# Two more neighbourhood heads mixed feature-major with split value weights in a two-block transformer kernel

## The chip, the cores and the metric

One NeuronCore of one Trainium2 chip runs the whole program. The metric is the device time of one execution in microseconds (us). The engines are TensorE (PE in the profile; its weight loads are PEld), VectorE (DVE), ScalarE (ACT), GpSimd (POOL) and SyncE (SP, which here only starts DMAs). Each engine runs its own instructions strictly in order and waits for the others by semaphores.

## The reference

The input is 256 tokens of width 1024. A first block and then a second one are computed in float32. Only the attention of the second block is touched here:

```python
u = rms_norm_2(h, mix_norm[l]);  z = u @ w_in[l]
qa, ka, va, qb, kb, vb, ga, gb = split(z)
ya = neighbourhood_attention_2d(qa, ka, va, rpb)       # 8 heads of 64: softmax(q k^T * scale + bias) v
yb = windowed_gqa_sink(rope(qb), rope(kb), vb, sink)   # 8 heads of 64, 2 key/value groups
merged = sigmoid(ga) * (ya @ w_branch_a) + sigmoid(gb) * (yb @ w_branch_b)
h = h + merged @ w_out
```

A neighbourhood head is thus a 256x256 score matrix, a softmax over each row, and the product of the probabilities with 256x64 values.

## The kernel before

**Numbers in two halves.** Float32 matmuls are done on values split into a high half (rounded to f32r by a copy on ACT) and a low half (the rest, subtracted on DVE). A product is then three f32r matmuls: high by high, high by low, low by high (`three`, lines 694 to 697). Weights arrive in panels of 1 MB in a ring of three (`raw`); ACT makes the high half of a panel (`hi`, line 1332), DVE the low half (`lo`, line 1802), each two panels ahead of PE. SP starts the load of a panel when DVE has made the low half of the panel three before it.

**The stretch.** The change lies in the projection stage of block 2, panels QKV2 to BR-1, which are called panels 0 to 16 here: QA2 = 0 and 4, KA2 = 1 and 5, VA2 = 2 and 3, KBVB = 6, QB = 7 and 8, GA2 = 9 to 12, GB2 = 13 to 16. Panels 0, 1 and 4 to 8 are of 48 matmuls 128x256 in two halves of 24; panels 2, 3 and 9 to 16 of 24 matmuls 128x512 with a break in the middle. The 16 attention heads are put between the halves of these panels by a table written by hand: slot 2p is the middle of panel p, slot 2p+1 its end (`places`, line 675). Head k has one slot for its scores (`score2`), a later one for turning its probabilities (`turn2_`) and a later one for its product with the values (`mix2`). In one slot PE does mix, turn and score in this order. Heads 0 to 7 are the neighbourhood heads, 8 to 15 the windowed ones.

**The two ways of a head.** `FV = 6` divides them. A head under FV: DVE masks the scores (`mask2`), ACT takes the exponential and the row sums (`exp2`), PE turns four 128x128 blocks of probabilities by float32 transposes, ACT copies them out of PSUM (`copy2`, into `probT2`), and PE does four float32 matmuls, turned probabilities as weights, 64 columns of values moving (line 1239; the profile counts each as two). The result is token-major; DVE takes the reciprocal of the sums and scales it into `atok2` (`norm2`). A head from FV on: DVE scales the probabilities by the reciprocal before they are turned (`scale2`, one slot behind the score's), ACT copies the turned ones as high half (`copy2` into `pth`), DVE makes the low half (`low_probs`), and PE does four f32r matmuls (line 1229) with 128 columns of weights, the 64 high and 64 low columns of the value side by side, and 256 columns of probabilities moving. The result is feature-major in two rows of 64 partitions; ACT copies the lower 64 (`low_rows`), DVE adds them to the upper ones (`norm2`). The mix waits for `low_probs` of its head.

**Order on DVE and ACT.** Both run through the panels too. DVE at n: take panel n-1 out of PSUM with its scale; the head work of slot (n-1, end): mask, low half of the probabilities, norm, scale; `lo(n+2)`; rope of panel n-1 where it was queries or keys of the windowed heads; at panel 8 the low halves of these keys (line 2394); the head work of slot (n, middle); at panel 8 then the low half of `vb` (line 2407). ACT at n, up to panel 9: `hi(n+2)`; high halves of queries; `swap` of the rope (line 1636), which waits until DVE has taken the panel out; then `low_rows` and `copy2` of slot (n-1, end), the exponentials of that slot, and `copy2` of slot (n, middle). From panel 10 on `low_rows` and `copy2` come first.

**Buffers and end.** `atok2` of heads 4 and 5 is turned by two transposes on PE after panel 12 (line 1296) into the third 128 rows of `midh`, `midl`; heads 6 and 7 need none, being written to `y3`.

Of the kernel before, what the change touches and what calls it, by code (L numbers as in the profile page):

```python
# [14 lines left out]
F32 = mybir.dt.float32  # L15
F32R = mybir.dt.float32r
ALU = mybir.AluOpType
ACT = mybir.ActivationFunctionType
AX_X = mybir.AxisListType.X

P = 128
T = 256
TT = T // P
D = 1024
KT = D // P
DH = 64
NH = 8
GR = 2
NC = 15
# [3 lines left out]
PW = 2048  # L33
R = 3
# [19 lines left out]
KBVB, QB, GA2, GB2 = QKV2 + 6, QKV2 + 7, QKV2 + 9, QKV2 + 13  # L54
# [45 lines left out]
def build(nc, a, out):  # L100
    ctx = ExitStack()
    with ctx:
        def sb(name, shape, dt=F32):
            return ctx.enter_context(nc.sbuf_tensor(name, shape, dt))
# [6 lines left out]
        wh_all = sb("wh", [P, R * PW + KT * 24], F32R)  # L111
        wl_all = sb("wl", [P, R * PW + KT * 24], F32R)
# [4 lines left out]
        midh = sb("midh", [P, 6, T], F32R)  # L117
        midl = sb("midl", [P, 6, T], F32R)
# [4 lines left out]
        xs = sb("xs", [P, TT, D])  # L123
        vec = sb("vec", [P, V_ALL])
        cw2 = sb("cw2", [P, 2, 2, DH])
        hid = sb("hid", [P, 2, 2, 2 * NC])
        hidt = sb("hidt", [P, 2 * CH])
        ssq = sb("ssq", [P, 2 * TT])
        wsq = sb("wsq", [P, 2 * TT])
# [19 lines left out]
        def carve(at, *shape):  # L149
            n = int(np.prod(shape))  # L150
            v = arena[:, at:at + n]
            names = "abcd"[:len(shape)]
            if len(shape) == 1:
                return v
            return v.rearrange("p (%s) -> p %s" % (" ".join(names), " ".join(names)),
                               **{k: s for k, s in zip(names, shape)})
# [18 lines left out]
        vblk = hidt[:, :].rearrange("p (g r d) -> p g r d", g=GR, r=4)  # L175
        pc = xsf[:, 1536:2048].rearrange("p (t h n) -> p t h n", t=TT, h=NH)
        pcT = carve(8224, 4, P)
        kcd = sb("kcd", [P, GR, 2 * NC])
        thr = sb("thr", [P, T])
        nth = carve(9760 + T, T)  # L180

# [6 lines left out]
        va = carve(10240, TT, NH * DH)  # L188
# [5 lines left out]
        pth, ptl = mrgl[:, 4:6, :], mrgl[:, 6:8, :]  # L194
        ylow = thr
        y3 = carve(12544, T)
        vns = midl[:, 4:6, :].rearrange("p k t -> p (k t)").rearrange("p (k h s d) -> p k h s d", k=TT, h=2, s=2)
        vbs = midh[:, 4:6, :].rearrange("p k t -> p (k t)").rearrange("p (k g s d) -> p k g s d", k=TT, g=GR, s=2)
        atok2 = carve(14336, TT, NH * DH)
        ybT = xs[:, 0, :].rearrange("p (k t) -> p k t", t=T)  # L200
# [20 lines left out]
        ps = [pair01[:, i, :] for i in range(2)] + [acc4[:, i, :] for i in range(4)] + [pair67[:, i, :] for i in range(2)]  # L221

        ident = cst[:, C_ID:C_ID + P]
# [99 lines left out]
        normed = sem("normed")  # L323
        atok_turned = sem("atok_turned")
        midh_ready = sem("midh_ready")
        midl_ready = sem("midl_ready")
# [317 lines left out]
        def head2(k):  # L644

            h = k % NH
            if k < NH:
                kh, kl = keys2(h // 4)
                return (qst[:, h, :], kh[:, h % 4, :], kl[:, h % 4, :],
                        [va[:, kt, DH * h:DH * (h + 1)] for kt in range(TT)] if h < FV else  # L650
                        [vns[:, kt, h - FV, :, :].rearrange("p s d -> p (s d)") for kt in range(TT)])
            g = h // 4
            return (qst[:, h, :], mrgl[:, g, :], mrgl[:, GR + g, :],
                    [vbs[:, kt, g, :, :].rearrange("p s d -> p (s d)") for kt in range(TT)])
# [7 lines left out]
            return ps[TURNED[0]][:, 0:T] if j == 3 else ps[3][:, 0:T]  # L662

        OUT_A = 5
        FV = 6
        KEY_BANKS = (KSKW % 2, 2)
        V_BANKS = (6, 5)
        LOW, HIGH, LAST = (0, 1), (4, 5), (6, 7)
# [8 lines left out]
        def places(slots):  # L677

            return {(QKV2 + at // 2, at % 2): k for k, at in enumerate(slots)}
# [1 line left out]
        SCORE_SLOTS = (5, 7, 9, 11, 13, 15, 17, 19, 21, 22, 23, 25, 26, 27, 29, 30)  # L681
        score_at = places(SCORE_SLOTS)
        scale_at = places([at + 1 for at in SCORE_SLOTS])
        turn_at = places((7, 9, 11, 13, 15, 17, 20, 22, 23, 25, 26, 27, 28, 30, 31, 32))
        mix_at = places((9, 11, 13, 15, 17, 19, 21, 23, 25, 26, 27, 28, 29, 31, 32, 33))


# [1 line left out]
        def _(pe):  # L689
# [274 lines left out]
            for c in range(2):  # L964
                m = high_first(1, c, ps[1][:, c * T:(c + 1) * T])
            m.then_inc(panel_done, 1)
            for n in range(KCVC, UPA):
# [3 lines left out]
                if n in CMPS:  # L971

                    s, u = CMPS.index(n) // 2, CMPS.index(n) % 2
                    if n == CMPS[0]:
                        pe.wait_ge(flatl_ready, 1)
                    h, l = pv(n, KT, wh), pv(n, KT, wl)
# [8 lines left out]
                elif n == VSVW:  # L985
                    h, l = vg(vg_h), vg(vg_l)
# [13 lines left out]
                else:  # L1000
                    for c in range(2):
                        out_ = ps[KEY_BANKS[c]][:, 0:T] if n == KSKW else bank1(n)[:, c * T:(c + 1) * T]
                        m = high_first(n, c, out_)
# [263 lines left out]
            for n in range(QKV2 + 1, BR):  # L1267
                split(n)
                free_bank2(n)
                if n in col2:  # L1270
                    for c in range(2):
                        m = feature_tile(n, KT, c, ps[n % 2][:, c * T:(c + 1) * T], acth, actl)
                        if c == 1:
                            m.then_inc(panel_done, 1)
                        elif n == QKV2 + 1:
                            spread(3)
                        heads2(n, c)
                else:
                    u = (n - (VA2 if n < GA2 else GA2)) % 4
                    token_panel(n, GATE2_BANKS[u // 2], acth, actl, 4 * (u % 2), u % 2 == 0, u % 2 == 1,  # L1280
                                lambda: heads2(n, 0)).then_inc(panel_done, 1)
                    heads2(n, 1)
                if n == QB:
                    pe.wait_ge(kv_evac, 1)
                    for tt in range(TT):
                        m = nc.tensor.transpose(ps[OUT_A][:, tt * P:(tt + 1) * P], vbT[:, tt * P:(tt + 1) * P], ident)
                    m.then_inc(vb_turned, 1)
                if n == GA2:
                    pe.wait_ge(normed, NH + 4)
                    pe.wait_ge(vb_ready, 1)  # L1290
                    turn_out(OUT_A, atok2, 0)
                if n == GA2 + 3:
                    pe.wait_ge(normed, NH + FV)
                    pe.wait_ge(midl_ready, 2)
                    for tt in range(TT):
                        m = nc.tensor.transpose(ps[OUT_A][:, tt * P:(tt + 1) * P], atok2[:, tt, 2 * P:3 * P], ident)
                    m.then_inc(atok_turned, 1)

            for u in range(2):
                for br, (ah, al) in enumerate(((midh, midl), (acth, actl))):  # L1300
# [14 lines left out]
        def _(act):  # L1315
# [368 lines left out]
            for n in range(QKV2, F2):  # L1684
# [42 lines left out]
                                             scale=rstd[:, tt:tt + 1]).then_inc(va_evac, 1)  # L1727
                if n == VA2 + 3:
                    act.wait_ge(va_evac, 2)
                    nc.scalar.activation(vns[:, :, :, 0, :], va[:, :, DH * FV:DH * NH].rearrange("p k (h d) -> p k h d", h=2),  # L1730
                                         ACT.Copy).then_inc(vnh_ready, 1)
                if n - 1 in (QB, QB + 1):
                    u = n - 1 - QB
# [17 lines left out]
                if n in (GA2 + 1, GA2 + 4):  # L1751
                    if n == GA2 + 1:
                        out_hi(midh, 0, OUT_A, 2)
                    else:
                        act.wait_ge(atok_turned, 3)
                        nc.scalar.activation(midh[:, 2, :], ps[OUT_A][:, 0:T], ACT.Copy)
                        act.wait_ge(normed, 2 * NH)
                        nc.scalar.activation(midh[:, 3, :], y3, ACT.Copy).then_inc(midh_ready, 1)
                if not grouped:
                    gates2(n)  # L1760
# [28 lines left out]
        def _(dve):  # L1789
# [498 lines left out]
            def norm2(k):  # L2288
                if k >= FV:

                    dve.wait_ge(ylow_ready, k - FV + 1)
                    to = y3 if k < NH else ybT[:, (k - NH) // 2, :]
                    nc.vector.tensor_tensor(to[own(k % 2)], ps[4][0:DH, 0:T], ylow[0:DH, :],
                                            ALU.add).then_inc(normed, 1)
                    return
                dve.wait_ge(mixed, NH + k + 1)
                o = k % 3
                c = coef[:, o, 0:TT]
                link(nc.vector.reciprocal(c, sums[:, o, 0:TT]))
                for tt in range(TT):  # L2300
                    m = nc.vector.tensor_scalar(atok2[:, tt, DH * k:DH * (k + 1)], ps[4][:, tt * DH:(tt + 1) * DH],
                                                coef[:, o, tt:tt + 1], None, ALU.mult)
                m.then_inc(normed, 1)
# [31 lines left out]
            for n in range(QKV2, F2):  # L2335
# [64 lines left out]
                    queries_lo(qbT, u, 5 + u)  # L2400
                if n == VA2 + 3:
                    dve.wait_ge(vnh_ready, 1)
                    nc.vector.tensor_tensor(vns[:, :, :, 1, :], va[:, :, DH * FV:DH * NH].rearrange("p k (h d) -> p k h d", h=2),
                                            vns[:, :, :, 0, :].bitcast(F32), ALU.subtract).then_inc(vn_ready, 1)
                if n == QB + 1:
                    dve.wait_ge(vbh_ready, 1)
# [2 lines left out]
                if n in (GA2 + 1, GA2 + 4):  # L2409
                    if n == GA2 + 1:  # L2410
                        out_lo(midl, midh, 0, OUT_A, 2)
                    else:
                        dve.wait_ge(midh_ready, 3)
                        nc.vector.tensor_tensor(midl[:, 2, :], ps[OUT_A][:, 0:T], midh[:, 2, :].bitcast(F32), ALU.subtract)
                        nc.vector.tensor_tensor(midl[:, 3, :], y3, midh[:, 3, :].bitcast(F32), ALU.subtract).then_inc(midl_ready, 1)

            residual(4, F2 - 1, then=V_F2)
# [73 lines left out]
```

## Time and profile before

| what | value |
|---|---|
| time, median of 3 runs | 952.55 us (952.55 to 952.73) |
| time of the profiled execution | 952.4 us |
| its span, first to last instruction | 950.5 us |
| mean granted TensorE clock | 0.999 |
| PE busy | 943.2 us (99%) |
| DVE busy | 665.9 us (70%) |
| ACT busy | 536.3 us (56%) |

A busy share is of the whole span; shares of single stretches differ much from it. The 1.9 us between the span and the time of the profiled execution lie outside the recorded instructions. All moments below are us from the start of the span.

### The profile page before, as it was taken

What the parts mean: (1) busy time and instruction counts of PE and PEld (TensorE: products, weight loads), DVE (VectorE), ACT (ScalarE), POOL (GpSimd) and SP (SyncE); (2) the same over time, 40 slices, a digit from 0 to 9 for tenths busy, and PEclk for the clock granted to TensorE, in tenths of its full rate; (3) what the DMA queues carried; (4) which work ended last, traced back from release to release, by engine and by line L of the source; (5) the groups of instructions that cost most, each with busy time, mean ns of one, the idle gap of its engine ahead of it and who ended that gap; (6) DMA issues with size and microseconds to landing.
All of it is one profiled execution on the core that took longest, in us unless ns stands there. A gap on an engine that the chain in (4) does not pass through costs nothing.

```text
span 950.5 us, 13952 instructions
## 1 busy us (share of the span) xinstructions
PE 943.2 (99%) x5400; PEld 826.7 (87%) x5400; DVE 665.9 (70%) x857; ACT 536.3 (56%) x691; POOL 62.3 (7%) x95
## 2 busy tenths in 40 slices
PE   9999999999999999999999999999999999999997
PEld 8999988888888888898888888999888898888886
DVE  7888869876655565688666666878887586665665
ACT  7687688535444444474454445679674465444544
POOL 1200000002000000022221000100100020000000
PEclk9999999999999999999999999999999999999999
DMA  9785335553756555547666655545435555655541
GB/s 304 227 244 168 110 123 182 199 178 118 273 181 197 199 177 184 187 160 243 207 207 204 201 177 177 181 137 170 133 133 178 177 192 185 220 178 183 194 153 44
DMA packets 119471, 173.14 MB, mean 182 GB/s; under 512 B 3168, under 2 KB 91488, under 8 KB 119424
## 3 DMA queue, kind: packets, MB, share of 16 engines
q1 hardware_dynamic: 117904, 168.41, 54.9%
q0 software_dynamic: 1376, 3.81, 1.4%
q8 instruction: 33, 0.54, 0.2%
q10 hardware_dynamic: 144, 0.26, 0.1%
q14 instruction: 14, 0.11, 0.0%
HBM read 171.42 MB, written 1.05 MB: 181 GB/s over the span
## 4 chain that ended last, share of the span: by engine, by line
PE 99%; DVE 0%; ACT 0%; issue 0%
PE pair L726 22%; PE pair L729 11%; PE acc L695 10%; PE acc L697 10%; PE acc L696 10%; PE pair L695 6%; PE pair L697 6%; PE pair L696 6%; PE pair L713 2%; PE pair L717 2%; PE pair L714 2%; PE acc L1065 1%; PE pair L923 1%; PE acc L1214 1%; PE acc L853 1%; PE pair L871 1%
## 5 line engine op out<-in xcount | busy, mean ns | idle before, releaser
L726 PE MATMUL pair<-actp,wh 128*128 128x512 f32 x912 | 292.8, 396 | 0.0
L1806 DVE TENSOR_TENSOR wl<-raw,wh 128x2048 fp32r<-128x2048 f32 x89 | 204.8, 2303 | 62.7 <-ACT wh L1338 62.7
L1338 ACT ACTIVATE wh<-raw 128x2048 fp32r<-128x2048 f32 x88 | 168.3, 1913 | 84.1 <-PE acc L697 84.1
L729 PEld LDWEIGHTS pair<-actp,wl 128*128 128x128 f32 x912 | 171.3, 188 | 40.0
L729 PE MATMUL pair<-actp,wl 128*128 128x256 f32 x912 | 179.2, 278 | 0.0
L1802 DVE TENSOR_TENSOR wl<-raw,wh 128x2048 fp32r<-128x2048 f32 x68 | 155.6, 2291 | 31.3 <-ACT wh L1332 30.9
L1332 ACT ACTIVATE wh<-raw 128x2048 fp32r<-128x2048 f32 x69 | 132.1, 1916 | 70.9 <-PE pair L697 27.4
L726 PEld LDWEIGHTS pair<-actp,wh 128*128 128x128 f32 x912 | 141.6, 189 | 1.4
L1553 ACT ACTIVATE arena<-pair 128x512 f32<-128x512 f32 x57 | 34.1, 598 | 170.8 <-PE pair L726 170.8
L695 PE MATMUL acc<-wh,midh 128*128 128x512 f32 x310 | 120.9, 390 | 0.0
L697 PE MATMUL acc<-wh,midl 128*128 128x512 f32 x310 | 120.6, 389 | 0.0
L696 PE MATMUL acc<-wl,midh 128*128 128x512 f32 x310 | 120.6, 389 | 0.0
L2153 DVE TENSOR_TENSOR arena<-pair,arena 128x512 f32<-128x512 f32 x57 | 39.4, 692 | 90.2 <-ACT arena L1553 90.2
L696 PEld LDWEIGHTS acc<-wl,midh 128*128 128x128 f32 x310 | 58.2, 188 | 12.2
L697 PEld LDWEIGHTS acc<-wh,midl 128*128 128x128 f32 x310 | 58.2, 188 | 12.2
L695 PEld LDWEIGHTS acc<-wh,midh 128*128 128x128 f32 x310 | 58.2, 188 | 10.7
L695 PE MATMUL pair<-wh,actp 128*128 128x512 f32 x160 | 63.6, 398 | 0.0
L697 PE MATMUL pair<-wh,actp 128*128 128x512 f32 x160 | 62.5, 391 | 0.0
L696 PE MATMUL pair<-wl,actp 128*128 128x512 f32 x160 | 62.4, 390 | 0.0
L2142 DVE TENSOR_TENSOR midl<-xs,midh 128x512 fp32r<-128x512 f32 x38 | 26.5, 698 | 23.1 <-ACT midh L1556 23.1
L713 PE MATMUL pair<-actp,wh 128*128 128x256 f32 x168 | 42.3, 290 | 0.0
L714 PE MATMUL pair<-actp,wh 128*128 128x256 f32 x168 | 41.1, 283 | 0.0
(375 smaller groups left out, 1452.3 us busy)
## 6 DMA issues: line engine op xcount, KB each, us to landing
raw<-in_w_in SPq DMA_DIRECT2D x35, 1024.0 KB, 5.2
raw<-in_mlp_w SPq DMA_DIRECT2D x32, 1024.0 KB, 5.2
raw<-in_ffn_w_gate SPq DMA_DIRECT2D x22, 1024.0 KB, 5.4
raw<-in_ffn_w_up SPq DMA_DIRECT2D x22, 1024.0 KB, 5.4
raw<-in_ffn_w_down SPq DMA_DIRECT2D x22, 1024.0 KB, 5.0
raw<-in_w_out SPq DMA_DIRECT2D x8, 1024.0 KB, 4.9
raw<-in_w_up_rnn SPq DMA_DIRECT2D x4, 1024.0 KB, 5.2
raw<-in_w_in SPq DMA_DIRECT2D x5, 512.0 KB, 5.5
```

The source lines that it names most:

```text
L695: nc.tensor.matmul(out_, lh, rh, start=start, stop=False, **kw)
L696: nc.tensor.matmul(out_, lh, rl, start=False, stop=False, **kw)
L697: return nc.tensor.matmul(out_, ll, rh, start=False, stop=stop, **kw)
L713: nc.tensor.matmul(out_, h[:, k, cs], acth[:, k, :], start=k == 0, stop=False)
L714: nc.tensor.matmul(out_, h[:, k, cs], actl[:, k, :], start=False, stop=False)
L726: return nc.tensor.matmul(bank[:, :].rearrange("p (u t) -> p u t", u=2), h[:, k, cs], actp[:, :, k, :], **kw)
L729: return nc.tensor.matmul(bank[:, 0:T], l[:, k, cs], acth[:, k, :], **kw)
L1332: nc.scalar.activation(to, src, ACT.Copy).then_inc(hi_ready, 1)
L1338: nc.scalar.activation(wh[:, slot(n), :], raw[:, slot(n), :], ACT.Copy).then_inc(hi_ready, 1)
L1802: nc.vector.tensor_tensor(to, src, high.bitcast(F32), ALU.subtract).then_inc(lo_ready, 1)
L1806: nc.vector.tensor_tensor(wl[:, slot(n), :], raw[:, slot(n), :], wh[:, slot(n), :].bitcast(F32), ALU.subtract).then_inc(lo_ready, 1)
L2153: return nc.vector.tensor_tensor(r, pair[:, :, 0:T], r, ALU.add)
```

## The change

FV becomes 4: heads 4 and 5 go the second way. Their values are split too: four copies on ACT and four subtractions on DVE at panel 5 in place of one each. Head 4's value weights lie in the unused last columns of `wh_all` and `wl_all`, head 5's in a new tile. Their turns move half a panel later, from slots 15 and 17 to 16 and 18; the slots of the scores and mixes stay. The result of the two heads goes to `y2`, so that the two transposes after panel 12 and their two waits go; ACT and DVE read `y2` in SBUF instead of a PSUM bank. `hid` and `kcd` of block 1 move into the shared arena.

```diff
-        FV = 6
+        FV = 4
-        turn_at = places((7, 9, 11, 13, 15, 17, 20, 22, 23, 25, 26, 27, 28, 30, 31, 32))
+        turn_at = places((7, 9, 11, 13, 16, 18, 20, 22, 23, 25, 26, 27, 28, 30, 31, 32))
+        y2 = carve(14592, T)
+        vn5 = sb("vn5", [P, TT, P], F32R)
+        vn4 = [v[:, R * PW:R * PW + P] for v in (wh_all, wl_all)]
...
                         [va[:, kt, DH * h:DH * (h + 1)] for kt in range(TT)] if h < FV else
-                        [vns[:, kt, h - FV, :, :].rearrange("p s d -> p (s d)") for kt in range(TT)])
+                        vn4 if h == 4 else [vn5[:, kt, :] for kt in range(TT)] if h == 5 else
+                        [vns[:, kt, h - 6, :, :].rearrange("p s d -> p (s d)") for kt in range(TT)])
...  (PE)
-                if n == GA2 + 3:
-                    pe.wait_ge(normed, NH + FV)
-                    pe.wait_ge(midl_ready, 2)
-                    for tt in range(TT):
-                        m = nc.tensor.transpose(ps[OUT_A][:, tt * P:(tt + 1) * P], atok2[:, tt, 2 * P:3 * P], ident)
-                    m.then_inc(atok_turned, 1)
...  (ACT, n == VA2 + 3; DVE subtracts in the same four pieces)
-                    nc.scalar.activation(vns[:, :, :, 0, :], va[:, :, DH * FV:DH * NH].rearrange("p k (h d) -> p k h d", h=2),
+                    for kt in range(TT):
+                        nc.scalar.activation(vn4[kt][:, 0:DH], va[:, kt, DH * 4:DH * 5], ACT.Copy)
+                    nc.scalar.activation(vn5[:, :, 0:DH], va[:, :, DH * 5:DH * 6], ACT.Copy)
+                    nc.scalar.activation(vns[:, :, :, 0, :], va[:, :, DH * 6:DH * NH].rearrange("p k (h d) -> p k h d", h=2),
                                          ACT.Copy).then_inc(vnh_ready, 1)
...  (ACT, n == GA2 + 4)
-                        act.wait_ge(atok_turned, 3)
-                        nc.scalar.activation(midh[:, 2, :], ps[OUT_A][:, 0:T], ACT.Copy)
                         act.wait_ge(normed, 2 * NH)
+                        nc.scalar.activation(midh[:, 2, :], y2, ACT.Copy)
...  (DVE, norm2)
-                    to = y3 if k < NH else ybT[:, (k - NH) // 2, :]
+                    to = (y2, y3)[k // 2 - 2] if k < NH else ybT[:, (k - NH) // 2, :]
```

## Rows read from the trace of the kernel before

**Rows 1.** The page: busy time, share of the span and instructions of each engine.
```profile
PE 943.2 (99%) x5400; PEld 826.7 (87%) x5400; DVE 665.9 (70%) x857; ACT 536.3 (56%) x691; POOL 62.3 (7%) x95
```

**Rows 2.** Waits of PE's weight loads, 590 to 760: total us, times, longest.
```profile
PEld acc L1199 <- issue: 0.4, 1, 0.4
```

**Rows 3.** Timeline of PE (start us, busy us, engine, line, operation), 645 to 669.
```profile
646.40 0.61 PE L1214 MATMUL acc<-cst,arena 128*128 128x128 f32 x4
646.76 0.36 PE L1199 MATMUL acc<-midh,mrgh 128*128 128x256 f32 x1
...
647.46 0.36 PE L695 MATMUL pair<-actp,wh 128*128 128x256 f32 x1
...
653.29 1.00 PE L1239 MATMUL acc<-arena 128*128 128x64 f32 x8
654.13 0.60 PE L1214 MATMUL acc<-cst,arena 128*128 128x128 f32 x4
...
655.05 0.39 PE L695 MATMUL pair<-wh,actp 128*128 128x512 f32 x1
...
660.52 1.00 PE L1239 MATMUL acc<-arena 128*128 128x64 f32 x8
...
668.28 0.64 PE L1229 MATMUL acc<-mrgl,midl 128*128 128x256 f32 x4
668.76 0.28 PE L1199 MATMUL acc<-mrgl,mrgh 128*128 128x256 f32 x1
```

**Rows 4.** Timeline of DVE, 630 to 672, with the idle time before an instruction.
```profile
630.74 0.69 DVE L2348 TENSOR_TENSOR arena<-pair,arena 128x512 f32<-128x512 f32 x1 [1.85 <-PE pair L697]
...
644.28 0.42 DVE L2327 TENSOR_TENSOR arena<-xs 128x256 f32<-128x256 f32 x1
645.76 0.69 DVE L2343 SCALAR_TENSOR_TENSOR arena<-pair,arena 128x512 f32<-128x512 f32 x1 [1.06 <-PE pair L697]
...
648.81 2.28 DVE L1802 TENSOR_TENSOR wl<-raw,wh 128x2048 fp32r<-128x2048 f32 x1
651.01 0.69 DVE L2324 TENSOR_TENSOR xs<-arena,cst 128x512 f32<-128x512 f32 x1
...
652.94 1.71 DVE L2394 TENSOR_TENSOR mrgl<-arena,mrgl 64x256 fp32r<-64x256 f32 x4
654.68 0.42 DVE L2407 TENSOR_TENSOR midh<-acc,midh 128x256 fp32r<-128x256 f32 x1
...
661.17 0.16 DVE L2276 RECIPROCAL coef<-sums 128x2 f32<-128x2 f32 x1
...
662.02 1.39 DVE L1896 TENSOR_TENSOR mrgh<-arena,mrgh 64x512 fp32r<-64x512 f32 x2
...
666.92 0.68 DVE L2285 TENSOR_TENSOR mrgl<-acc,mrgl 128x512 fp32r<-128x512 f32 x1
...
671.19 0.41 DVE L2293 TENSOR_TENSOR arena<-acc,thr 64x256 f32<-64x256 f32 x1
```

**Rows 5.** Timeline of ACT, 631 to 669, with the idle time before an instruction.
```profile
631.46 2.59 ACT L1702 ACTIVATE midh<-arena 64x512 fp32r<-64x512 f32 x4 [3.20 <-DVE arena L2348]
...
648.39 2.55 ACT L1636 ACTIVATE arena<-arena 32x512 f32<-32x512 f32 x4
...
651.25 0.59 ACT L1625 ACTIVATE arena<-acc 128x512 f32<-128x512 f32 x1
...
653.55 1.92 ACT L1332 ACTIVATE wh<-raw 128x2048 fp32r<-128x2048 f32 x1 [0.59 <-PE pair L697]
...
656.65 2.56 ACT L1636 ACTIVATE arena<-arena 32x512 f32<-32x512 f32 x4
...
668.96 0.38 ACT L1631 ACTIVATE thr<-acc 64x256 f32<-64x256 f32 x1 [2.13 <-PE acc L1229]
```

**Rows 6.** Stretches of 1 us at the end: length, busy of each engine, PEclk.
```profile
944.00:945.00 1.00, 0.49 (x5) 0.29 (x3) 0.85 (x2) 0.97 (x4) 0.35 (x1) 1.00 0.00 0
...
948.00:949.00 1.00, 0.00 (x0) 0.00 (x0) 0.00 (x0) 0.00 (x0) 0.00 (x0) 0.75 1.03 391
```

More of the change, by code:

```diff
@@ L125, in build @@
         cw2 = sb("cw2", [P, 2, 2, DH])
-        hid = sb("hid", [P, 2, 2, 2 * NC])
         hidt = sb("hidt", [P, 2 * CH])
@@ L177, in build @@
         pcT = carve(8224, 4, P)
-        kcd = sb("kcd", [P, GR, 2 * NC])
+        hid = carve(15392, 2, 2, 2 * NC)
+        kcd = carve(15512, GR, 2 * NC)
         thr = sb("thr", [P, T])
@@ L2402, in _ @@
                     dve.wait_ge(vnh_ready, 1)
-                    nc.vector.tensor_tensor(vns[:, :, :, 1, :], va[:, :, DH * FV:DH * NH].rearrange("p k (h d) -> p k h d", h=2),
+                    for kt in range(TT):
+                        nc.vector.tensor_tensor(vn4[kt][:, DH:P], va[:, kt, DH * 4:DH * 5], vn4[kt][:, 0:DH].bitcast(F32), ALU.subtract)
+                    nc.vector.tensor_tensor(vn5[:, :, DH:P], va[:, :, DH * 5:DH * 6], vn5[:, :, 0:DH].bitcast(F32), ALU.subtract)
+                    nc.vector.tensor_tensor(vns[:, :, :, 1, :], va[:, :, DH * 6:DH * NH].rearrange("p k (h d) -> p k h d", h=2),
                                             vns[:, :, :, 0, :].bitcast(F32), ALU.subtract).then_inc(vn_ready, 1)
@@ L2413, in _ @@
                         dve.wait_ge(midh_ready, 3)
-                        nc.vector.tensor_tensor(midl[:, 2, :], ps[OUT_A][:, 0:T], midh[:, 2, :].bitcast(F32), ALU.subtract)
+                        nc.vector.tensor_tensor(midl[:, 2, :], y2, midh[:, 2, :].bitcast(F32), ALU.subtract)
                         nc.vector.tensor_tensor(midl[:, 3, :], y3, midh[:, 3, :].bitcast(F32), ALU.subtract).then_inc(midl_ready, 1)
```

## The prediction

> **What bounds the kernel now.** First the page's busy shares: PE is busy for 99% of the span [rows 1], so a microsecond of PE work saved or waited for anywhere is a microsecond of the whole. Then PE's waits over the attention stage: the only entry is 0.4 us in one piece that nothing releases [rows 2]; no head makes PE wait now. Then the timelines of PE, DVE and ACT side by side, since the change gives DVE and ACT more work here and puts a new wait into PE. The reader is to see two things. PE's head work sits between panel matmuls without a hole [rows 3]. On DVE, from 648.81 on, `lo`, rope (651.01), the low key halves (652.94) and `vb`'s low half (654.68) stand end to end, with no idle time shown before any of them [rows 4]. ACT in the same panels holds two swaps of 2.55 us, at 648.39 and 656.65 [rows 5]. DVE's 70% over the span [rows 1] hides this full stretch.
>
> **PE work, removed and moved.** An old mix takes 653.29 to 654.13 = 0.84 us, a new one 668.28 to 668.76 = 0.48 us [rows 3]: two heads save 2 x 0.36 = 0.72. The four transposes of a turn take 646.40 to 646.76 = 0.36 [rows 3]; the two transposes that go are half of that, 0.18. The moved turns are the same work. Where float32 work hands over to f32r the first matmul is longer (0.36 against 0.28 for the same shape [rows 3]); two such switches go (a new mix is followed by scores of its own kind) and two come (a turn alone in the middle of a panel), so I cost them at nothing, bounds -0.2 to +0.2. Sum for PE: -0.9 us, bounds -0.7 to -1.1.
>
> The Trainium skill bears on this term ("TensorE: Matmul & The Clock Gate", section "Back-to-back issue gap"). Its formula for isolated matmuls, columns / 2.4 plus 2.5 ns, with its floor of 25 ns, would give the old mix 8 x 29 ns = 0.23 us and the new one 4 x 109 ns = 0.44, so the change would cost 0.4 us in place of saving 0.7. The trace disagrees for the small ones: 0.84 us for eight is 105 ns each [rows 3]. The same section says that the formula counts too little at few columns because every matmul has its weight load, and by that the trace agrees. The rows are used.
>
> **Work hidden at panel 5.** The four value copies and four subtractions replace one each. Nearest rows: 0.38 us for an ACT copy of 256 columns [rows 5], 0.41 for a DVE operation of 256 [rows 4]; eight operations of at most that size are under 3.3 us, six of them new; as the pieces have 64 to 128 columns I take 0.6 us more on ACT and 0.5 on DVE. Behind them DVE idles 1.85 us until 630.74 [rows 4] and ACT 3.20 until 631.46 [rows 5]. Cost 0; were that cover gone, the next mask and `copy2` would be up to a microsecond late, three panels ahead of the heads in question. Moving `hid` and `kcd`, and reading `y2` from SBUF instead of PSUM, costs nothing either: same operations, far from PE's next need. Bounds of all these -0.1 to +0.3.
>
> **The scale of head 4.** `scale2(4)` comes on DVE behind rope's last piece (644.28 + 0.42 = 644.70) and takes 661.17 to 662.02 = 0.85. DVE idles 1.06 there before 645.76 [rows 4]: hidden, with 0.2 to spare.
>
> **First new wait: mix of head 4 at slot 17.** When PE gets there: panel 8 starts at 647.46 now and its end is 653.29 [rows 3]. The turn leaves slot 15 (-0.36) and comes into the middle of panel 8 with its switch (+0.44): 653.37. What it waits for is `low_probs(4)`. On ACT, the swap from 648.39 ends at 650.94 as now, and then exponential and `copy2(4)` stand in the other order; both are done when ACT now falls idle, 653.55 - 0.59 = 652.96 [rows 5]. That is in time. DVE is not: the low half of the probabilities comes behind the low key halves in program order, so not before 654.68, where `vb` now starts [rows 4]. Can DVE be earlier? Its mask of head 5 comes 0.36 earlier, as the turn ahead of its scores is gone, but rope then waits for ACT's swap, over at 650.94, and rope starts at 651.01 already [rows 4, 5]. So DVE's time stands. `low_probs` takes 0.68 [rows 4]: done 655.36, with an allowance of 0.1 for handing over 655.46. **PE stands for 2.1 us.** Bounds 1.4 (0.3 lost or gained in either chain, twice) to 2.8. Behind the waiting mix on PE are the scores of head 6 and all of panel 9.
>
> **Second new wait: mix of head 5 at slot 19.** PE: 655.46, mix 0.48, scores 0.48 (the same four matmuls of 256 columns), panel 9 660.52 - 655.05 = 5.47 [rows 3], turn with switch 0.44: 662.3. DVE: behind `low_probs(4)` (next start 655.28) come `scale2(5)` 0.85 and `vb`'s low half, 0.34 to the next start: 656.5; then taking out panel 8, 0.65: 657.1. Only now may ACT swap (now it starts at 656.65, behind other ACT work, so ACT is ready): 657.2 + 2.56 = 659.75 [rows 5]. Behind the swap in ACT's order stands `low_rows(4)`, 0.38 [rows 5]: 660.15. DVE's `norm2(4)` waits for that, and behind it on DVE are queued `lo` of panel 11, rope and `low_probs(5)`: 660.15 + 0.4 + 2.2 (648.81 to 651.01) + 1.93 (651.01 to 652.94) + 0.68 = 665.35 [rows 4], handed over 665.45. **PE stands for 3.1 us.** The wait of DVE for `low_rows` is the dear part, about 2.3 us (657.8 after the mask, to 660.15): an old head's norm needs PE alone. Bounds 2.0 to 4.2, as six terms add.
>
> **What is late next.** PE's lag is now 665.45 - 660.52 - 0.36 = 4.6 us. DVE's: `scale2(6)`, now at 661.17, comes at 665.3, a lag of 4.1. As DVE lags less than PE, and `low_probs(6)` ends now at 667.60 for a mix at 668.28 [rows 3, 4], 0.7 to spare, head 6 and all behind it keep their distances. Queries and high halves move by no more. No third wait (bounds 0 to 0.4). Later SP's load of panel 14 starts some 4 us later, behind `lo` of panel 11; two panels of distance cover it, and if they didn't, PE would wait for up to 4 us more.
>
> **Sum**, against the profiled execution, 952.4 (its span 950.5 and 1.9 around it): -0.9 + 2.1 + 3.1 = +4.3, so 956.7. The median before is 0.15 above that execution: **956.8**.
>
> **Rivals.**
> A, *no new wait; only PE's saving is left*. It decides at one point: whether `low_probs(4)` is done by 653.4 and `low_probs(5)` by PE's 660.2. For it: the exponential and the copy are done at 652.96. Against it: DVE's row at 654.68 and its program order. Price: -0.9, so 951.6, not slower.
> B, *only the first wait*. `norm2(4)` would have to find `low_rows(4)` done, so DVE reaches `low_probs(5)` at 657.1 + 0.7 + 0.4 + 2.2 + 1.93 = 662.3, done 663.1: a wait of 0.8 in place of 3.1, 954.5, or with none 953.7. Against it: the 2.56 us swap ahead of `low_rows`.
> C, *the waits cool the clock*. PE's last work ends near 944.5, and the granted clock still reads 1.00 up to 948 and 0.75 in the microsecond after it [rows 6], so it fell to the 1.2 GHz level after some 3.5 us of standing; my second wait is 3.1. Price: a panel of 5.47 us [rows 3] at half rate is +5.5 at most, I take half: 959.5. The Trainium skill states such a rule, under "HAM oscillation — how this bites in real kernels" of "TensorE: Matmul & The Clock Gate": TensorE that stands idle long enough for data drops back to the lower clock and starts its next work cold. By the page a single wait could bring this time; by the rows here, mine is just short of what did.
> D, *faster by more than PE's saving*, through some wait in the panels not seen in rows 2: none speaks for it.
>
> **Chances.** Forecast 0.70 (955.3 to 958.5), B 0.10, A 0.08, C 0.07, D and the unforeseen 0.05. Range 953.4 to 959.2: it takes in B and the lower half of C, and leaves A and the dearest of C out. A measurement of this kernel can tell 0.2%, 1.9 us, from no change: faster means under 950.7, slower over 954.4. Faster 0.06 (D, and part of A), same 0.14 (A, half of B), slower 0.80.
>
> **What the changed profile would show.** PE's waits: a line for `pth`/`ptl` behind L2285 on DVE, twice, about 2 and 3 us, ahead of the mixes of heads 4 and 5; the four matmuls of those mixes at 0.48 a head. DVE: `low_probs` near 654.7 directly behind the low key halves, and an idle time of about 2.3 us before `norm2(4)`, released by ACT. ACT: no time lost before its second swap but that until 657.2. If PE shows no wait, DVE's order was read wrongly and A holds; if the second wait is missing, the chain through swap and `low_rows` is wrong; if PEclk dips near 665, C.

## The result, and the profile after

The changed kernel takes 956.56 us (median of 6 runs, 956.32 to 957.92), the kernel before 952.55 (6 runs, 952.27 to 953.18): a ratio of 1.0043, 95% interval 1.0032 to 1.0053. It is slower by 4.0 us; 956.8 was predicted. The profiled execution took 956.65 us with a span of 954.9, 4.4 more than the span before. In this kernel's listing the lines of PE have moved down by four: 699 to 701 for `three`, 1218 the turns, 1233 the f32r mixes; those of ACT's head work have moved up by two (`swap` 1634, `low_rows` 1629, `copy2` 1623).

The page, first part, against [rows 1]: PE's busy time grows by 1.0 us, though its work has become less, and there are ten rows fewer.

```profile
PE 944.2 (99%) x5390; PEld 827.2 (87%) x5390; DVE 668.7 (70%) x864; ACT 536.9 (56%) x696; POOL 61.6 (6%) x95
```

Waits of PE's weight loads, 590 to 760 (engine and line, what released it: us in total, times, longest), against the single line of [rows 2]. The two new ones stand ahead of the mixes of heads 4 and 5. Their releaser is named "issue" here. The timelines name DVE for the second; for the first it is inferred from the times, as `low_probs(4)` ends at 654.76 + 0.69 = 655.45 and the mix starts at 655.56.

```profile
PEld acc L1233 <- issue: 3.8, 2, 2.2
PEld acc L1203 <- issue: 0.4, 1, 0.4
```

Timeline of PE (start us, busy us, engine, line, operation, idle before), which answers to [rows 3]. The end of panel 8, mix and scores, the first half of panel 9, its turn, its end, the mix of head 5 with its scores, and the mix of head 6:

```profile
653.29 0.28 PE L701 MATMUL pair<-actp,wl 128*128 128x256 f32 x1
655.56 0.77 PE L1233 MATMUL acc<-mrgl,wh 128*128 128x256 f32 x2 [1.99 <-issue]
656.12 0.63 PE L1233 MATMUL acc<-mrgl,wl 128*128 128x256 f32 x2
...
657.40 0.63 PE L699 MATMUL pair<-wh,actp 128*128 128x512 f32 x1
...
660.83 0.60 PE L1218 MATMUL acc<-cst,arena 128*128 128x128 f32 x4
...
663.79 0.39 PE L701 MATMUL pair<-wh,actp 128*128 128x512 f32 x1
665.42 0.71 PE L1233 MATMUL acc<-mrgl,vn 128*128 128x256 f32 x4 [1.24 <-DVE mrgl L2285]
...
672.84 0.64 PE L1233 MATMUL acc<-mrgl,midl 128*128 128x256 f32 x4
```

The reader is to see three things: the mix of head 4 starts 2.15 us after its turn has come (653.29 + 0.12, one matmul's distance), the mix of head 5 1.4 us after (663.79 + 0.23), and between them PE is slow: from 657.40 to the turn it takes 3.43 us for what took 2.75 where the clock was high (e8 below, 656.22 to 658.97). At the mix of head 6 the lag behind [rows 3] is 672.84 - 668.28 = 4.56 us.

Timeline of DVE, which answers to [rows 4]. `scale2(4)` stands in the old idle time; `low_probs(4)` (L2285) is directly behind the low key halves; `norm2(4)` idles DVE for 1.71 us until ACT's `low_rows`; `low_probs(5)` closes the chain:

```profile
644.71 0.16 DVE L2276 RECIPROCAL coef<-sums 128x2 f32<-128x2 f32 x1
...
645.85 0.69 DVE L2343 SCALAR_TENSOR_TENSOR arena<-pair,arena 128x512 f32<-128x512 f32 x1 [0.33 <-PE pair L701]
...
653.02 1.71 DVE L2394 TENSOR_TENSOR mrgl<-arena,mrgl 64x256 fp32r<-64x256 f32 x4
654.76 0.69 DVE L2285 TENSOR_TENSOR mrgl<-acc,mrgl 128x512 fp32r<-128x512 f32 x1
...
660.13 0.42 DVE L2293 TENSOR_TENSOR arena<-acc,thr 64x256 f32<-64x256 f32 x1 [1.71 <-ACT thr L1629]
660.47 2.27 DVE L1802 TENSOR_TENSOR wl<-raw,wh 128x2048 fp32r<-128x2048 f32 x1
...
664.59 0.68 DVE L2285 TENSOR_TENSOR mrgl<-acc,mrgl 128x512 fp32r<-128x512 f32 x1
```

Timeline of ACT, which answers to [rows 5]: the second swap waits for DVE, `low_rows(4)` follows it.

```profile
657.14 2.55 ACT L1634 ACTIVATE arena<-arena 32x512 f32<-32x512 f32 x4 [0.41 <-DVE arena L2343]
659.71 0.38 ACT L1629 ACTIVATE thr<-acc 64x256 f32<-64x256 f32 x1
```

Stretches of 1 us (length, busy of PE, PEld, DVE, ACT and POOL, PEclk, DMA share, GB/s). The third figure from the end is the granted clock: 0.50 is the 1.2 GHz level, 1.00 the 2.4 GHz level, and a figure between them is the mean of a microsecond in which it changed. The 0.73 puts the fall near 655.46, at the very end of PE's first wait; the clock was back in the course of 658 to 659.

```profile
654.00:655.00 1.00, 0.00 (x0) 0.00 (x0) 0.96 (x3) 1.00 (x1) 0.00 (x0) 1.00 1.05 410
655.00:656.00 1.00, 0.44 (x2) 0.47 (x3) 0.96 (x4) 1.00 (x2) 0.00 (x0) 0.73 0.35 133
656.00:657.00 1.00, 1.00 (x7) 1.00 (x7) 1.00 (x3) 0.72 (x2) 0.00 (x0) 0.50 0.00 0
...
658.00:659.00 1.00, 1.00 (x4) 0.78 (x3) 0.41 (x4) 0.99 (x2) 0.00 (x0) 0.56 0.00 0
```

### The profile page after: what moved, and what is told of

It is laid out like the page before. It is cut to its first block, busy times and chain, and to the rows that moved or that the text cites. A ratio compares the mean times of both kernels' runs of the same rounds, so it can differ in the third digit from the quotient of the medians.

```text
span 954.9 us, 13945 instructions
## 1 busy us (share of the span) xinstructions
PE 944.2 (99%) x5390; PEld 827.2 (87%) x5390; DVE 668.7 (70%) x864; ACT 536.9 (56%) x696; POOL 61.6 (6%) x95
## 4 chain that ended last, share of the span: by engine, by line
PE 96%; DVE 2%; ACT 1%; DMA 1%; issue 0%; SPq 0%
PE pair L730 22%; PE pair L733 11%; PE acc L699 10%; PE acc L701 10%; PE acc L700 10%; PE pair L699 5%; PE pair L701 5%; PE pair L700 5%; PE pair L721 2%; PE pair L717 2%; PE pair L718 2%; PE acc L1069 1%; PE pair L927 1%; PE acc L857 1%; PE acc L1218 1%; DMA raw<-in_w_in 1%
```

## The experiments

The theory: PE's time at the mix of head 5 is set by one chain on DVE and ACT (low key halves, `low_probs(4)`, taking out panel 8, second swap, `low_rows(4)`, `norm2(4)`, `lo`, rope, `low_probs(5)`), whatever PE did before. The rivals: the fall of the clock is a part of the loss; DVE simply has too much work, in any order. Each kernel was timed in five rounds, beside the kernel before on the same chip: 952.30 us beside e1 to e4, 952.39 beside e5 to e8, 952.60 beside e9.

**e1: the first wait filled with matmuls that nobody reads.**

```diff
             def mix2(k):
                 vt = head2(k)[3]
+                if k == 4:
+                    for _ in range(5):
+                        nc.tensor.matmul(ps[6][:, 0:T], ident, cst[:, C_COS:C_COS + T], start=True, stop=True)
```

> The changed kernel with five float32 matmuls 128x256, whose result nobody reads, put on PE ahead of the mix of head 4, so that PE works through most of its first wait of 2.1 us and its clock does not fall. Chain theory: what sets the end is the chain on DVE and ACT up to the low half of head 5's probabilities (near 665.3), whatever PE does before; the second wait grows from 1.4 to about 3 us, PEclk stays at 1.0, the time stays at 956.5 (956.2 to 957.0). Clock theory: the stretch at 1.2 GHz from 655.4 to 658.6 is part of the loss; without it the time falls by about 1.5 us to 955.0.

Measured: 957.79 us, ratio 1.0052 (1.0039 to 1.0066). The clock stayed high through the first wait, and as the chain theory has it, the mix of head 5 starts at the same moment all the same (665.23), now after 2.75 us of idle. But the time is 0.8 above the range I gave. One of the five executions took 956.30, the others 957.69 to 958.17; the trace is of one of these. PE's timeline and the clock behind this second wait:

```profile
665.23 0.71 PE L1236 MATMUL acc<-mrgl,vn 128*128 128x256 f32 x4 [2.75 <-DVE mrgl L2288]
...
674.22 0.64 PE L1236 MATMUL acc<-mrgl,midl 128*128 128x256 f32 x4
```

```profile
665.00:666.00 1.00, 0.77 (x6) 0.80 (x7) 0.93 (x5) 0.03 (x1) 0.00 (x0) 1.00 1.00 385
666.00:667.00 1.00, 1.00 (x9) 1.00 (x7) 0.99 (x2) 1.00 (x2) 0.00 (x0) 0.61 0.96 373
667.00:668.00 1.00, 1.00 (x5) 0.81 (x4) 0.97 (x5) 1.00 (x1) 0.00 (x0) 0.50 0.05 16
```

The clock now falls here, with PE at work again, and nothing behind it takes the loss up: from the mix of head 5 to that of head 6 it is 8.99 us (674.22 - 665.23), in the changed kernel 7.42 (672.84 - 665.42).

**e8: both waits filled.** As e1, and six more such matmuls into a free bank ahead of the mix of head 5.

```diff
+                if k == 5:
+                    pe.wait_ge(qb_evac, 2)
+                for _ in range({4: 5, 5: 6}.get(k, 0)):
+                    nc.tensor.matmul(ps[6 if k == 4 else 0][:, 0:T], ident, cst[:, C_COS:C_COS + T], start=True, stop=True)
```

> The changed kernel with unread matmuls in both waits (five ahead of head 4's mix, six ahead of head 5's), so that the clock falls behind neither. Chain theory: PE starts the mix of head 5 at the same moment as in the changed kernel and goes on at the full clock: 956.5 (956.1 to 956.9), 1.3 less than with the first wait alone filled (957.8). If the added 1.3 us there came from something else than the clock: 957.8 again.

Measured: 956.20 us, ratio 1.0039 (1.0026 to 1.0053), inside the range; the clock reads 1.00 in both places.

```profile
655.19 0.47 PE L1237 MATMUL acc<-mrgl,wh 128*128 128x256 f32 x2
...
656.22 0.40 PE L699 MATMUL pair<-wh,actp 128*128 128x512 f32 x1
658.97 0.60 PE L1218 MATMUL acc<-cst,arena 128*128 128x128 f32 x4
...
665.06 0.71 PE L1237 MATMUL acc<-mrgl,vn 128*128 128x256 f32 x4
...
672.47 0.64 PE L1237 MATMUL acc<-mrgl,midl 128*128 128x256 f32 x4
```

Two things follow. One fall of the clock with nothing behind it to hide it costs 957.79 - 956.20 = 1.59 us, and the rows say the same (8.99 - 7.41 = 1.58). And with no fall at all the loss is still 956.20 - 952.39 = 3.8 us: the fall in the changed kernel was all but free (956.56 - 956.20 = 0.36 us, or 0.2 when each is taken against the kernel before beside it). There the mix of head 4, scores and half a panel took 660.83 - 655.56 = 5.27 us against 658.97 - 655.19 = 3.78 here; these 1.5 us were taken from the second wait, not added to the end.

**e2: head 4's lower rows ahead of the second swap on ACT.**

```diff
+                if n == GA2:
+                    heads2_turned(n - 1, 1)
                 if n - 1 in (QB + 1, QB + 2):
...
-                if not grouped:
+                if not grouped and n != GA2:
                     heads2_turned(n - 1, 1)
```

> The changed kernel with the copy of head 4's lower rows ahead of the rope's second swap on ACT, in place of behind it. Chain theory: norm2(4) no longer idles DVE for 1.7 us, low_probs(5) is done near 663.5 in place of 665.3, and PE, which arrives near 664.0 with the low clock behind it, doesn't wait a second time: 956.5 - 1.4 = 955.1. Work theory (DVE simply has too much to do in this stretch, and the order is of no account): no change, 956.5.

Measured: 954.16 us, ratio 1.0020 (1.0011 to 1.0029), 2.4 less than the changed kernel. `norm2(4)` no longer idles DVE, `low_probs(5)` starts 2.6 us earlier, and PE comes later than it:

```profile
657.31 0.41 DVE L2295 TENSOR_TENSOR arena<-acc,thr 64x256 f32<-64x256 f32 x1
...
661.98 0.68 DVE L2287 TENSOR_TENSOR mrgl<-acc,mrgl 128x512 fp32r<-128x512 f32 x1
```

```profile
663.72 0.64 PE L1233 MATMUL acc<-mrgl,vn 128*128 128x256 f32 x4
```

The same work in another order, so the work rival falls for this part. The gain is larger than I said, by 0.9. The executions fall into two groups, and the mean granted clock of each execution tells them apart: six of 953.93 to 954.16 us with 0.998 to 1.000, and five of 954.63 to 954.89, all with 0.996. The profiled one is of the upper group; in its trace PEclk is 0.50 from 657 to 659. Some 3 us at half rate lower the mean of such a span by about 0.002 (an estimate from these figures), so in the faster group the clock seems not to have fallen behind the same wait of 2 us. The groups are 0.8 us apart, less than a whole fall costs by e8, since PE without the fall reaches the mix before `low_probs(5)` is done (e5 below shows 0.55 us of wait there).

**e3: head work of panel 8's middle ahead of the low key halves on DVE.**

```diff
+                heads2(n, 0)
                 if n == QB + 1:
                     dve.wait_ge(kst_hi, 9)
...
                     m.then_inc(kst_ready, 1)
-                heads2(n, 0)
```

> The changed kernel with the head work of the middle of panel 8 on DVE (low half of head 4's probabilities, scaling of head 5) ahead of the low key halves. The first wait shrinks from 2.1 to about 0.5 us. Chain theory: nothing is gained, as the panel is taken out, swapped and roped at the same moments as before; the second wait grows to 4 us or more: 956.5, and up to 958 if the longer wait cools the clock for what comes after it. Rival, the waits count singly: 956.5 - 1.6 - 1.5 (no low clock) = 953.4.

Measured: 958.14 us, ratio 1.0062 (1.0048 to 1.0076), 0.1 above what I expected at most: mending the first wait alone makes it worse. PE's idle times are 0.32 and 4.49 us, and the mix of head 5 starts where it did:

```profile
653.66 0.48 PE L1233 MATMUL acc<-mrgl,wh 128*128 128x256 f32 x2 [0.32 <-issue]
...
665.28 0.76 PE L1233 MATMUL acc<-mrgl,vn 128*128 128x256 f32 x4 [4.49 <-DVE mrgl L2285]
```

The clock fell behind the longer wait (0.91 in 665 to 666, 0.50 in 666 to 667), for the same 1.6 us as in e1 (8.98 us from the mix of head 5 to that of head 6). Waits do not count singly; the last one in the chain holds them all.

**e4: the turns of heads 4 and 5 back in slots 15 and 17.**

```diff
-        turn_at = places((7, 9, 11, 13, 16, 18, 20, 22, 23, 25, 26, 27, 28, 30, 31, 32))
+        turn_at = places((7, 9, 11, 13, 15, 17, 20, 22, 23, 25, 26, 27, 28, 30, 31, 32))
```

> The changed kernel with the turns of heads 4 and 5 where they were before, at the ends of panels 7 and 8. Chain theory: low_probs(4) then stands on DVE ahead of lo, rope and keys and idles it until ACT, behind its swap, has copied (652); everything behind it is 2 to 3 us later, the turn of head 5 waits on PE for its scaling for some 6 us, and a further wait comes at head 6: 959 to 961. Rival, the later turns are what costs, because they shorten the time between turn and mix: 954 or less.

Measured: 960.07 us, ratio 1.0079 (1.0065 to 1.0093). As expected, `low_probs(4)` idles DVE, and the turn of head 5 waits on PE for `scale2(5)`. A line of DVE and one of PE:

```profile
651.69 0.69 DVE L2285 TENSOR_TENSOR mrgl<-acc,mrgl 128x512 fp32r<-128x512 f32 x1 [3.60 <-ACT mrgl L1623]
```

```profile
659.63 0.69 PE L1218 MATMUL acc<-cst,arena 128*128 128x128 f32 x2 [5.87 <-DVE arena L2279]
```

So the later turns are worth 3.5 us (960.07 - 956.56, not measured side by side, but beside kernels before of 952.30 and 952.55). The expected third wait, at head 6, is not there.

**e5: e2 and e1 together.** Both diffs above.

> The changed kernel with head 4's lower rows copied ahead of the second swap and the five unread matmuls ahead of the mix of head 4. PE keeps its clock through the first wait and reaches the mix of head 5 about 1.4 us earlier than in the kernel with the lower rows first alone; the low half of head 5's probabilities is then the later of the two by some 0.6 us. Chain theory with the clock as a cost of its own: 954.16 - 1.4 + 0.6 = 953.4 (953.0 to 953.8). If the low clock costs nothing here either: 954.2.

Measured: 954.38 us, ratio 1.0020 (1.0011 to 1.0029): a miss by 1 us, and no gain over e2's median. The steps in the trace are those named (clock 1.00 throughout, 0.55 us of idle ahead of the mix of head 5), and the span is 952.6 against 953.1 in e2's profiled execution:

```profile
663.27 0.71 PE L1236 MATMUL acc<-mrgl,vn 128*128 128x256 f32 x4 [0.55 <-DVE mrgl L2290]
```

What was wrong is the base: I took 1.4 us of clock loss off e2's median, and the median lies in e2's faster group, whose mean granted clock shows no such loss. Taken off the slower group the sum is 954.85 - 1.4 + 0.6 = 954.05, and eight of the eleven executions here took 953.94 to 954.47. The other three took 955.01 to 955.47 at the same mean clock, 0.999; what they lost stays open.

**e6: e2 and e3 together.**

> The changed kernel with both orders mended: head 4's lower rows ahead of the second swap on ACT, and the head work of panel 8's middle ahead of the low key halves on DVE. First wait 0.3 us; the chain to the low half of head 5's probabilities is as long as with the lower rows first alone (done near 662.7), so PE waits 2 us there. Chain theory: 952.3 - 0.9 + 0.3 + 2.0 = 953.7 without a fall of the clock behind the wait, up to 955.1 with one. Rival, the two gains add: 954.16 - 1.5 = 952.6 or less.

Measured: 955.39 us, ratio 1.0029 (1.0018 to 1.0039), 0.3 above the upper of the two values I gave. The idle times are 0.32 and 2.06 us as the chain has it, and the clock falls behind the second (0.78 in 663 to 664, then 0.50):

```profile
663.05 0.77 PE L1233 MATMUL acc<-mrgl,vn 128*128 128x256 f32 x4 [2.06 <-DVE mrgl L2287]
```

Seven of the eight executions took 955.31 to 955.76 us at a mean granted clock of 0.996 or 0.997; one took 954.01 at 1.000, near the 953.7 of a kernel whose clock does not fall. The two gains do not add: the second makes the first worse by 1.2 us.

**e7: the stretch in order of due time.** The main steps of the edit (`LO_LATER` is panels 10 and 11 of the stretch):

```diff
 (ACT, n == GA2, behind hi)
+                    heads2_turned(n - 1, 1)
+                    act.wait_ge(qb_evac, 2)
+                    swap(swq[:, 1, :], qbT[:, 2:4, :].rearrange("p a t -> p (a t)"))
+                    heads2_turned(n, 0)
...
 (ACT, n == GA2 + 1: heads2_turned(n, 0) ahead of heads2_scored(n - 1, 1))
...
 (DVE)
-                if n < F2 - 1:
+                if n < F2 - 1 and n not in LO_LATER:
                     lo(n + 2)
+                if n == GA2:
+                    low_probs(5)
...
-                if n == QB + 1:
+                if n == GA2 + 1:
                     dve.wait_ge(kst_hi, 9)
...
+                    queries_lo(qbT, 0, 5)
                 heads2(n, 0)
+                if n == GA2 + 1:
+                    queries_lo(qbT, 1, 6)
+                if n in LO_LATER:
+                    lo(n + 2)
```

> The changed kernel with the work of panels 8 to 11 in an order by due time. DVE: head work of panel 8's middle without the low key halves, these and the first low query halves only at panel 10; low half of head 5's probabilities ahead of the rope; lo of panels 12 and 13 behind the head work of panels 10 and 11. ACT: head 4's lower rows, the second swap and head 5's copy ahead of the high query halves. Nothing is left out. Chain theory: waits of PE of 0.3 us at the first mix and near none after, so that only the saving of PE work is left: 952.3 - 0.9 + 0.4 = 951.8 (951.4 to 952.6). Work theory: the added 2.5 us on DVE must come out somewhere in a full stretch: 954 or more.

Measured: 953.49 us, ratio 1.0010 (1.0001 to 1.0019). This is a miss for both theories: 0.9 above the chain theory's range and 0.5 below the work theory's. The waits at the mixes of heads 4 and 5 are gone but for 0.3 us, yet a new one has come, 1.3 us ahead of the scores of head 9, for the mask of head 8. I had put `lo` of panel 12 (L1811) ahead of that mask (L1898):

```profile
669.52 2.29 DVE L1811 TENSOR_TENSOR wl<-raw,wh 128x2048 fp32r<-128x2048 f32 x1
...
672.33 0.47 DVE L1898 CUSTOM_DVE_ANT_0 arena<-acc,cst,small 128x256 f32<-128x256 f32 x1
```

Waits of PE's weight loads (some of those not shown are of 0.2 to 0.4 us):

```profile
PEld acc L1204 <- DVE nmax L1898: 1.3, 1, 1.3
PEld acc L1234 <- issue: 0.5, 1, 0.5
```

**e9: the same, with three more steps moved.**

```diff
                 if n < F2 - 1 and n not in LO_LATER:
                     lo(n + 2)
+                if n == GA2 + 2:
+                    lo(n + 1)
...
-                if n == GA2 + 1:
+                if n == GA2 + 2:
                     queries_lo(qbT, 1, 6)
-                if n in LO_LATER:
                     lo(n + 2)
```

> The reordered kernel with three more steps moved on DVE: lo of panel 12 from the end of panel 10's work to behind the masks and norms of its last slot (where DVE idles for its scores), the low query halves of heads 12 to 15 and lo of panel 13 behind the head work of panel 11. In the first reordering PE waited 1.3 us ahead of the scores of head 9, for the mask of head 8, which stood behind these. Chain theory: that wait goes, the 0.3 us at the mix of head 4 stays: 952.4 - 0.9 + 0.3 = 951.8 (951.6 to 952.3), 1.7 less than the first reordering. Work theory: the wait turns up somewhere else, 953 or more.

Measured: 951.94 us against 952.60 of the kernel before, ratio 0.9994 (0.9985 to 1.0003), inside the chain theory's range. All work of the changed kernel is in it, DVE 668.1 us busy against 668.7. What is left of waits:

```profile
PEld acc L1234 <- issue: 0.5, 1, 0.5
PEld acc L1204 <- issue: 0.4, 1, 0.4
PEld acc L1219 <- DVE arena L2288: 0.2, 1, 0.2
PEld acc L1234 <- DVE xs L2302: 0.2, 1, 0.2
```

This is 4.6 us less than the changed kernel; the work rival falls altogether. Against the kernel before the interval takes in 1: it cannot be called faster, and is not slower.

## Why the prediction was right

**PE work, -0.9.** No run measures the saving alone; the rows of e9, where no clock falls, show its parts:

```profile
653.63 0.47 PE L1234 MATMUL acc<-mrgl,wh 128*128 128x256 f32 x2 [0.32 <-issue]
...
654.17 0.28 PE L1204 MATMUL acc<-midh,mrgh 128*128 128x256 f32 x1
...
660.59 0.64 PE L1234 MATMUL acc<-mrgl,vn 128*128 128x256 f32 x4
661.06 0.28 PE L1204 MATMUL acc<-midh,mrgh 128*128 128x256 f32 x1
```

The mix of head 5 takes 0.47 us as predicted, that of head 4 takes 0.54, as it opens with longer matmuls behind its short wait. The two save about 0.65 in place of 0.72, and the whole term comes to some -0.8, inside its bounds. Times are too coarse for it: e9 is 0.66 below the kernel before, but its interval reaches from 1.4 below to 0.3 above, and it has some 0.7 us of waits that the kernel before has not.

**First wait, 2.1.** Measured 2.15 us. Each link came as written: `low_probs(4)` at 654.76 (654.68 + 0.08, by which this whole execution is late), rope bound by ACT's swap, ACT idle again at 653.06.

**Second wait, 3.1.** The end of the chain was right, 664.59 + 0.68 = 665.27 (665.35), and with it the sum. The wait itself was 1.4 us, since PE came 1.6 us later than I had it: this is the step that failed, and it belongs to rival C. I put a fall of the clock behind the second wait only, and left it out of the sum, because the only one in the rows came after some 3.5 us of standing. Those rows, read closely, speak of a longer time still: 0.75 is the mean of 948 to 949, so the fall came near 948.5, 4 us after PE's last work [rows 6]. In the changed kernel it came behind the first wait, of 2 us. The level was right (0.50), the price lower than the 2.7 us taken: 1.6, by e1 against e8. That it did not reach the end is the second wait's doing, which the prediction did not reckon with. That the time came out to 0.2 us in spite of it was luck: behind the second wait, as in e1 and e3, the same fall gave 957.8 to 958.1. By the rule of the Trainium skill that the prediction named ("TensorE: Matmul & The Clock Gate", section "HAM oscillation — how this bites in real kernels") TensorE falls back in a gap that is long enough and starts its next work at the lower clock. The trace agrees that the next work started there (PEclk 0.50 in 656 to 657); but the gap that brought it, 2.15 us, is shorter than the page has it, and here the measurement decides.

**DVE's wait for the lower rows.** Predicted 2.3 us, measured 1.71: DVE's mask of head 6 came later, with PE slowed in its scores (in e3, where the clock was still high there, DVE idles 2.34). e2 shows what it does to the end.

**What is late next.** Right: PE's lag is 4.56 us at the mix of head 6, predicted 4.6, and 4.4 at the end of the span. No third wait.

**Work at nothing.** Right: the value pieces took 0.22 to 0.42 us each in idle time of DVE, which fell from 1.85 to 1.38 us.

**Rivals.** A (no new wait), B (only the first) and D (faster by more) fell. e2 and e9 show the orders from which B and A hold: with `low_rows(4)` ahead of the swap 954.16 us came for the 953.7 to 954.5 of B, and with DVE and ACT in order of due time 951.94 for the 951.6 of A.

## What to carry to other kernels

When a kernel's bottleneck engine never waits, as PE here, price a change by the order of the other engines' programs, not by their busy share: write down when the waited-for instruction gets its turn there, and follow the chain to the last wait. Mend a chain from its last wait back; mending the first alone only moved the wait here, and made it dearer. Moving work that is due late behind work that is due soon, with nothing taken out, was worth 4.6 us here (956.56 to 951.94).

## What the runs showed of the hardware

TensorE's granted clock fell to the 1.2 GHz level in or just behind waits of 2 to 6 us: 2.15 us in the changed kernel, 2.06 in e6, 2.75 in e1, 4.49 in e3, 5.87 in e4. Behind waits of 2 us it did not fall in every execution: by the mean granted clock it seems to have stayed up in six of e2's eleven and in one of e6's eight. In e1 it still read 1.00 when PE had taken up work again, and fell in the microsecond after. In e4 it still read 1.00 more than 4 us into the standing:

```profile
657.00:658.00 1.00, 0.00 (x0) 0.00 (x0) 0.97 (x4) 0.86 (x2) 0.00 (x0) 1.00 0.86 295
658.00:659.00 1.00, 0.00 (x0) 0.00 (x0) 0.92 (x4) 0.40 (x1) 0.00 (x0) 0.89 1.04 408
```

One fall cost 1.6 us where no later wait took it up (e1 against e8; 1.4 between the two kinds of execution of e6), and 0.2 to 0.4 us, which is hardly clear of the noise, where one did. Matmuls that nobody reads, put into the wait, kept the clock from falling (e1 at the first wait, e5, e8). They bought little here: e8 is 0.4 us below the changed kernel, e5 0.2 above e2, and e1, with the first wait alone filled, 1.2 above the changed kernel.
